# A transformer pair's modulation vectors: from products on TensorE to row sums on ScalarE

## The reference, cut to what matters

```python
c_act = jax.nn.silu(c)                      # (1, 1024)
for l in range(2):
    mod = c_act @ w_ada[l] + b_ada[l]       # (1, 1024) @ (1024, 6144)
    sh1, sc1, g1, sh2, sc2, g2 = jnp.split(mod, 6, axis=-1)
    h = rms_norm(x, ln1_g[l]) * (1.0 + sc1) + sh1
    ...
    x = x + g1 * (merged @ w_out[l])
    ...
```

## Time and profile before

| what | value |
|---|---|
| median of 3 runs | 1462.53 us (1462.26 to 1467.37) |
| the profiled execution | 1466.21 us |
| its span | 1464.4 us |
| TensorE products busy | 1392.3 us, 95% |
| VectorE busy | 872.1 us, 60% |
| ScalarE busy | 802.6 us, 55% |
| GpSimd busy | 547.2 us, 37% |
| granted TensorE clock, mean | 0.974 of full speed |

### The profile page before, as it was taken

How to read it: one execution, slowest core, us unless ns; L and a number is a source line. 1 busy time by engine, 2 the same in 40 slices (tenths; PEclk the granted TensorE clock), 3 DMA queues, 4 the chain that set the end, 5 groups by cost and what they waited for, 6 DMA issues and landing times.

```text
span 1464.4 us, 25774 instructions
## 1 busy us (share of the span) xinstructions
PE 1392.3 (95%) x11032; PEld 1347.1 (92%) x11032; DVE 872.1 (60%) x1047; ACT 802.6 (55%) x954; POOL 547.2 (37%) x249
## 2 busy tenths in 40 slices
PE   6999899998999979999999998999999999899997
PEld 5989899998999979999988997999988998899996
DVE  4865666755555467666759767434445876734443
ACT  4655577765676457777536544454324554455431
POOL 5000288885331337988606000564000600066300
PEclk9999999999899989999999999999999999999998
DMA  7433677777654466777624444555542543355550
GB/s 261 142 115 115 222 275 261 256 292 305 224 207 159 140 239 241 264 262 269 229 103 170 169 145 144 178 191 179 192 150 80 199 155 144 137 192 190 177 198 29
DMA packets 40002, 278.22 MB, mean 190 GB/s; under 512 B 4432, under 2 KB 4560, under 8 KB 8144
## 3 DMA queue, kind: packets, MB, share of 16 engines
q1 hardware_dynamic: 32976, 226.23, 43.8%
q10 hardware_dynamic: 6912, 50.33, 8.9%
HBM read 275.50 MB, written 1.05 MB: 189 GB/s over the span
## 4 chain that ended last, share of the span: by engine, by line
PE 87%; DVE 6%; ACT 3%; POOL 2%; issue 2%; DMA 0%; DVEq 0%; ACTq 0%; SPq 0%; POOLq 0%
PE bank L738 22%; PE bank L740 22%; PE bank L739 22%; PE bank L703 3%; PE bank L704 2%; PE bank L710 2%; DVE low L1421 2%; PE bank L952 1%; PE bank L722 1%; PE bank L724 1%; PE bank L723 1%; PE bank L772 1%; PE bank L759 1%; DVE h L1554 1%; ACT high L1068 1%
## 5 line engine op out<-in xcount | busy, mean ns | idle before, releaser
L1421 DVE TENSOR_TENSOR low<-raw,high 128x2048 fp32r<-128x2048 f32 (+4 forms) x222 | 510.8, 2304 | 306.0 <-ACT high L1068 303.7
L738 PE MATMUL bank<-op_high,low 128*128 128x256 f32 x1904 | 549.1, 288 | 3.3 <-DVE low L1421 3.3
L739 PE MATMUL bank<-op_low,high 128*128 128x256 f32 x1904 | 540.5, 284 | 0.0
L740 PE MATMUL bank<-op_high,high 128*128 128x256 f32 x1904 | 540.4, 284 | 0.0
L1068 ACT ACTIVATE high<-raw 128x2048 fp32r<-128x2048 f32 (+4 forms) x222 | 406.3, 1831 | 155.2 <-PE bank L740 143.6
L738 PEld LDWEIGHTS bank<-op_high,low 128*128 128x128 f32 x1904 | 367.4, 193 | 8.8 <-DVE low L1421 4.4
L739 PEld LDWEIGHTS bank<-op_low,high 128*128 128x128 f32 x1904 | 367.3, 193 | 2.8 <-issue 2.4
L740 PEld LDWEIGHTS bank<-op_high,high 128*128 128x128 f32 x1904 | 367.1, 193 | 0.0
L738 PE MATMUL bank<-act_high,low 128*128 128x256 f32 x864 | 242.7, 281 | 0.0
L740 PE MATMUL bank<-act_high,high 128*128 128x256 f32 x864 | 242.0, 280 | 0.0
L739 PE MATMUL bank<-act_low,high 128*128 128x256 f32 x864 | 240.6, 278 | 0.0
(11 more groups left out here) (288 smaller groups left out, 1910.6 us busy)
## 6 DMA issues: line engine op xcount, KB each, us to landing
raw<-stream SPq DMA_DIRECT2D x198, 1024.0 KB, 4.8
adaw<-ada ACTq DMA_DIRECT2D x48, 1024.0 KB, 6.2
raw<-stream SPq DMA_DIRECT2D x10, 768.0 KB, 4.5
raw<-stream SPq DMA_DIRECT2D x10, 512.0 KB, 3.6
x<-xT SPq DMA_DIRECT2D x1, 1024.0 KB, 5.1
out<-h SPq DMA_DIRECT2D x1, 1024.0 KB, 3.9
raw<-stream SPq DMA_DIRECT2D x2, 384.0 KB, 3.3
consts<-consts_d SPq DMA_DIRECT2D x1, 672.0 KB, 14.1
```

What stands on the lines that cost most here:

```text
L738: pe.matmul(o, wl[:, w], oh[:, k, :], start=one, stop=False, skip_group_check=True)
L739: pe.matmul(o, wh[:, w], ol[:, k, :], start=False, stop=False, skip_group_check=True)
L740: mm = pe.matmul(o, wh[:, w], oh[:, k, :], start=False, stop=end, skip_group_check=True)
L1421: dve.tensor_tensor(low[m % SPLIT][:, 0:w], raw[m % RAW][:, 0:w], high[m % SPLIT][:, 0:w], ALU.subtract).then_inc(S["low_ready"], 1)
```

## The change

The modulation's weights are laid out the other way round on the host: a partition holds one output feature, and a portion two groups of 128 output features by all 1024 input features. The condition's row is loaded once, broadcast to all partitions (`crow`), and silu is applied to the whole row at step 1. GpSimd multiplies each half of a portion by `crow`. Two steps behind, ScalarE copies each half onto itself with a row sum (`accum_out`), which gives 128 finished outputs at a time, in SBUF. VectorE adds the bias from there. The products `ada_sum` on TensorE are gone, with their two borrowed banks.

```diff
-        adas = [sb(f"adas{i}", [P, D], F32, adaln) for i in range(2)]
+        crow = sb("crow", [P, D], F32, adaln)
...
                 if ADA_SUM_AT[seg] == step[0]:
-                    st_("ada_sum", seg), st_("mod", seg)
+                    st_("mod", seg)
             for p in range(48):
+                if ADA_AT[p] + 2 == step[0]:
+                    st_("ada_acc", p)
                 if ADA_AT[p] == step[0]:
+                    if p == 0:
+                        st_("cond_silu")
                     st_("ada", p)
...
             if l == 0:
-                st_("ada_load", 0)
+                st_("ada_cond"), st_("ada_load", 0)
...
-            def ada_sum(seg):
-
-                pe.wait_ge(S["ada_added"], 4 * (seg + 1))
-                bank = MOD_BANK[seg]
-                claim(bank)
-                for b in range(8):
-                    mm = pe.matmul(ps[bank][:, 0, b:b + 1], adas[seg % 2][:, b * P:(b + 1) * P],
-                                   col("ones", 0, 1), start=True, stop=True)
-                mm.then_inc(S["ada_sum"], 1)
-                free_after[bank] = (S["mod_ready"], seg + 1)
...
-            def ffn_in(l):
-                if l == 0:
-                    act.activation(cact[:], col("c"), ACT.Silu).then_inc(S["c_silu"], 1)
+            def ada_cond(_):
+                act.dma_start(crow[:], cond.to_broadcast([P, D])).then_inc(S["c_in"], 16)
+
+            def cond_silu(_):
+                act.wait_ge(S["c_in"], 16)
+                act.activation(crow[:], crow[:], ACT.Silu).then_inc(S["c_silu"], 1)
 
             def ada_load(a):
                 if a >= 3:
-                    act.wait_ge(S["ada_added"], a - 2)
+                    act.wait_ge(S["ada_summed"], 2 * (a - 2))
...
-            def ada_(a):
-
-                act.wait_ge(S[f"ada_in{a % 3}"], 16 * (a // 3 + 1))
-                if a == 0:
-                    act.wait_ge(S["c_silu"], 1)
+            def ada_acc(a):
+
+                l, part, q = a // 24, a // 4 % 6, a % 4
+                w = adaw[a % 3]
                 for i in range(2):
-                    k = 2 * (a % 4) + i
-                    ins = act.activation(adaw[a % 3][:, i, :], adaw[a % 3][:, i, :], ACT.Copy, scale=cact[:, k:k + 1])
-                ins.then_inc(S["ada_scaled"], 1)
+                    act.wait_ge(S["ada_scaled"], 2 * a + i + 1)
+                    m = 8 * part + 2 * q + i
+                    act.activation(w[:, i, :], w[:, i, :], ACT.Copy, accum_out=mod[:, l, m:m + 1])\
+                        .then_inc(S["ada_summed"], 1)
...
                 m = mod[:, l, 8 * part:8 * part + 8]
-                dve.wait_ge(S["ada_sum"], seg + 1)
-                dve.tensor_tensor(m, ps[MOD_BANK[seg]][:, 0, 0:8], col("b_ada", 8 * seg, 8), ALU.add)\
+                dve.wait_ge(S["ada_summed"], 8 * (seg + 1))
+                dve.tensor_tensor(m, m, col("b_ada", 8 * seg, 8), ALU.add)\
                     .then_inc(S["mod_ready"], 1)
...
             def ada_(a):
 
-                seg, part = a // 4, a % 4
-                acc, w = adas[seg % 2], adaw[a % 3]
-                pool.wait_ge(S["ada_scaled"], a + 1)
-                if part == 0:
-                    if seg >= 2:
-                        pool.wait_ge(S["ada_sum"], seg - 1)
-                    pool.tensor_tensor(acc[:], w[:, 0, :], w[:, 1, :], ALU.add).then_inc(S["ada_added"], 1)
-                    return
-                pool.wait_ge(S["ada_added"], a)
-                link(pool.tensor_tensor(acc[:], w[:, 0, :], acc[:], ALU.add))
-                pool.tensor_tensor(acc[:], w[:, 1, :], acc[:], ALU.add).then_inc(S["ada_added"], 1)
+                w = adaw[a % 3]
+                pool.wait_ge(S[f"ada_in{a % 3}"], 16 * (a // 3 + 1))
+                if a == 0:
+                    pool.wait_ge(S["c_silu"], 1)
+                for i in range(2):
+                    pool.tensor_tensor(w[:, i, :], w[:, i, :], crow[:], ALU.mult).then_inc(S["ada_scaled"], 1)
```

More of the change, by code:

```diff
@@ L190, in columns @@
                     ("od_q_gain", 1), ("od_k_gain", 1), ("conv", 2 * 44 * 4), ("ln1", 16), ("ln2", 16),
-                    ("b_ada", 96), ("q_norm", 6), ("kv_norm", 4), ("pool_scale", 8), ("final_g", 8), ("c", 8),
+                    ("b_ada", 96), ("q_norm", 6), ("kv_norm", 4), ("pool_scale", 8), ("final_g", 8),
                     ("w_kr", 512)):
@@ L194, in columns, with build @@
     return where, sizes
-def build(nc, xT, stream, ada, consts_d, params_d, positions, out):
+def build(nc, xT, stream, ada, cond, consts_d, params_d, positions, out):
     CH, _ = linear_chunks()
@@ L232, in build @@
         gmod = sb("gmod", [P, 2, 2, KB])
-        cact = sb("cact", [P, KB])
         small = sb("small", [P, 64])
@@ L336, in build @@
             diff_scores diff_max diff_exp diff_w diff_turned diff_copied diff_pv mix_ready
-            conv_init conv_done silu_done act_mul act_high act_low c_silu ada_in0 ada_in1 ada_in2 ada_scaled ada_added ada_sum mod_ready
+            conv_init conv_done silu_done act_mul act_high act_low c_in c_silu ada_in0 ada_in1 ada_in2 ada_scaled ada_summed mod_ready
             dil_scores dil_max dil_exp dil_w dil_turned dil_copied dil_pv dv_ready
@@ L428, in build @@
         ADA_SUM_AT = [ADA_AT[4 * seg + 3] + 3 for seg in range(12)]
-        MOD_BANK = [NB if 34 <= at < 52 else OB for at in ADA_SUM_AT]
         step = [0]
@@ L445, in conv_stages @@
         def conv_stages(l):
-            st_("norm", 2 * l + 1), st_("ffn_in", l)
+            st_("norm", 2 * l + 1)
             if l == 0:
-                st_("ada_load", 0)
+                st_("ada_cond"), st_("ada_load", 0)
             for j in range(11):
@@ L1041, in _ @@
                           gla_kv=gla_kv, diff_p=diff_p, dil_p=dil_p, dil_p2=dil_p2, mla_p=mla_p,
-                          gla_o=gla_o, diff_s=diff_s, diff_t=diff_t, dil_s=dil_s, dil_t=dil_t, ada_sum=ada_sum, kr=kr_,
+                          gla_o=gla_o, diff_s=diff_s, diff_t=diff_t, dil_s=dil_s, dil_t=dil_t, kr=kr_,
                           krot=krot, wide=wide, qrot=qrot, mla_s=mla_s, mla_t=mla_t)
@@ L1393, in _ @@
                           turns=turns, lam=lam, ar=ar_, la=la_, la_exps=la_exps, ket=ket,
-                          gated=gated, mix=mix, diff_s=diff_s, diff_t=diff_t, dil_s=dil_s, dil_t=dil_t, ffn_in=ffn_in,
-                          silu=silu, ada=ada_, ada_load=ada_load, act=act_, act2=act2, kr=kr_, wide=wide, pool_split=pool_split, y=y_, heads=heads,
+                          gated=gated, mix=mix, diff_s=diff_s, diff_t=diff_t, dil_s=dil_s, dil_t=dil_t, ada_cond=ada_cond, cond_silu=cond_silu,
+                          silu=silu, ada_acc=ada_acc, ada_load=ada_load, act=act_, act2=act2, kr=kr_, wide=wide, pool_split=pool_split, y=y_, heads=heads,
                           after_heads=after_heads,
@@ L1972, in lay_params @@
                       ("q_norm", "q_norm_g_2"), ("kv_norm", "kv_norm_g_2"), ("pool_scale", "pool_scale_2"),
-                      ("final_g", "final_g_2"), ("c", "c_2")):
+                      ("final_g", "final_g_2")):
         put(name, by_feature(i[src]))
@@ L2012 @@
     xT = np.ascontiguousarray(np.asarray(i["x"])[0].T.reshape(KB, P, TOK).transpose(1, 0, 2))
-    wa = np.asarray(i["w_ada_2"]).reshape(2, 4, 2, P, 6, D)
+    wa = np.asarray(i["w_ada_2"]).reshape(2, D, 6, 4, 2, P).transpose(0, 2, 3, 5, 4, 1)
     arrays = {
-        "xT": xT, "stream": lay_stream(i), "ada": np.ascontiguousarray(wa.transpose(0, 4, 1, 3, 2, 5)).reshape(-1),
+        "xT": xT, "stream": lay_stream(i), "ada": np.ascontiguousarray(wa).reshape(-1),
+        "cond": np.ascontiguousarray(np.asarray(i["c_2"]).reshape(1, D)),
         "consts_d": shape_constants(), "params_d": lay_params(i),
```

## The result

The changed kernel takes 1473.31 us (median of 5 runs, 1472.68 to 1473.43) against 1462.53 (5 runs, 1462.08 to 1467.37): a ratio of 1.0061, 95% interval 1.0042 to 1.008. The ratios in this document are those of the means (here 1473.1 and 1464.2). The forecast was 1443.5 us with a range of 1438 to 1453. The profiled execution took 1472.68 us (span 1470.8).

The account below looks back on a forecast made before the run. TensorE, with 87% of the chain, was taken as the bound. 22.0 + 0.7 - 0.1 - 0.4 - 2.0 - 1.0 = 19.2 us saved from 1462.5 gives 1443.3, stated as 1443.5 us, range 1438 to 1453.

Parts of the forecast that it names:

- The 12 blocks: TensorE's 12 blocks of thin `ada_sum` products, 1.78 us each plus or less waits around them: removing them saves 22.0 us.
- the clock: TensorE's granted clock, 0.79 in the 8 us from 395 on, recovers: 0.7 us saved, bounds 0 and 1.5.
- 0.1 and 0.4: Losses from ScalarE's sums coming two steps later: net 0.1 us at step 33's norm, 0.4 us at step 44.
- A product's own cost: A GpSimd product in the modulation must cost what one of its sums does, 2.41 us.
- Rival D: A GpSimd product costs more than a sum, so turns in the `up` steps set TensorE's pace: 1492 us, chance 0.04.
- ScalarE's sum: ScalarE's copy with row sum takes about 1052 ns plus 195 ns to read the accumulator: no change of load.
- The turns: GpSimd and VectorE alternate in `up` steps, falling at worst 0.32 us behind per period; late `act_low` costs TensorE 2.0 us.
- for all such places: ScalarE, held by GpSimd's products before its sums, delays the next splits and so TensorE: 1.0 us, bounds 0 and 9.
- 12 tiny instructions, off the path: VectorE's additions to the modulation, reading the sums from SBUF and not PSUM, were taken to cost nothing.
- no longer waits for ScalarE there: At step 33, GpSimd finishes before VectorE's normalization, which it delayed by 0.9 us; ScalarE's 1.0 us lateness nets 0.1.
- A: GpSimd and VectorE saturate their turns in the `up` steps, costing 6.2 us and not 2.0: 1447.7 us, chance 0.14.
- B: ScalarE's waits reach TensorE where portions stand closest, steps 24-26 and 80-84: 9.6 us, not 1.0; 1452 us, chance 0.14.

Follow-up runs that it names:

- experiment 5: The changed kernel at the old tile addresses, each of GpSimd's 96 products cut to one column of 1024: 1439.24 us, ratio 0.9817 to the kernel before.
- experiment 1: The changed kernel with three unused tiles that put every later tile back at its old address: 1467.55 us, ratio 1.0013 to the kernel before.
- experiment 6: The changed kernel at the old tile addresses, each GpSimd product cut into two of 512 columns: 1459.93 us, ratio 0.9955 to the kernel before.
- experiment 4: The changed kernel with GpSimd's products of each portion held until ScalarE's split of that portion's step: 1475.88 us, ratio 1.0068 to the kernel before.
- experiment 10: The kernel before with unused tiles added and `mod` moved ahead of `x`, putting operands 448 bytes from the weights modulo 512: 1440.32 us, ratio 0.9825.

## Why the prediction was wrong

**Step by step.**
- The 12 blocks and the clock, 22.0 + 0.7, less 0.1 and 0.4, together 22.2: right as far as the runs can tell. With the products reduced to one column the kernel is 26.0 us faster than the kernel before beside it, with 4 to 5 us in it that may be the old sums' own turns (experiment 5). In the `up` and `down` steps the terms agree with the traces to 1.1 us each. L952 is gone, and so are the waits at 395 and 434.
- A product's own cost, like a sum's: right. Its shortest was 2.35 us. Rival D was wrong in its mechanism.
- ScalarE's sum: right, 1048 and 189 ns where 1052 and 195 were taken. Its waits for products, 8.5 us in experiment 1, are not what costs the time (experiment 6).
- The turns: **the step that failed**. The text weighed GpSimd against VectorE over "a period of two `up` steps", 11.84 against 11.52 us, and gave the result 2.0 us for a late `act_low` (bounds 0 and 6.2). That was roughly right: the two waits for `act_low` are 3.6 us in the changed kernel and 3.4 in experiment 1, and the 2 x 22 `up` steps themselves lose 0.6. But the `down` steps were never weighed that way. The working followed one chain of waits there, at the tightest place, found 2 us of slack and took 1.0 us "for all such places, with bounds 0 and 9"; the load over the whole stretch, 42.3 + 23.7 us of turns within the 62, was not added up. There GpSimd has no other work, so nothing holds its products apart, and each keeps VectorE out for its length. The two terms, 3.0 us together, measure 28.3 for all of the products (experiment 5 against 1), and 23 to 24 if the 4 to 5 us are the old sums' turns, which the forecast had in its starting point.
- The same step took the rule of turns from splits alone. The traces show it for the additions of squares and to the modulation too, which have both inputs in SBUF, and the short ones pay most: 0.43 us become 2.5. The kernel before had such additions already (four of 2.5 to 2.6 us), so it could have been read there. One kind was named and priced at nothing ("12 tiny instructions, off the path"): the addition to the modulation, whose input this change moves from PSUM to SBUF, takes 1.62 us on the mean where it took 0.16.
- What had kept the turns apart was, as far as the traces tell, the old dependence; no run shows it, and the hold of experiment 4 didn't bring it back. GpSimd waited 108.8 us (line 1838) and 37.1 us (line 1835) in the kernel before for ScalarE's scaling, and in the `down` steps VectorE worked in those gaps. The forecast saw those waits only as waits to be removed, in the sentence that GpSimd "no longer waits for ScalarE there". Afterwards it waits for transfers alone, 97.3 us, mostly where nothing presses.
- The sum had no term for the addresses: that all other work keeps its pace was assumed without a word. It was 6 to 7 us (experiment 1), outside any part of the kernel that the diff touches.

**The books.** In ratios to the kernel before, of a mean of 1464.2 us: the removal, with the old sums' turns, -0.0183 or -26.8 us (experiment 5; forecast -22.2), the products +0.0196 or +28.7 (experiment 1 less 5; forecast +3.0), the layout +0.0048 or +7.0 (the changed kernel less experiment 1; no term in the forecast). Together +8.9, from 1464.2 to 1473.1. The three parts are differences of the same runs and so add up by construction; each is good to 2 or 3 us.

**The chances.** 0.90 went to a gain, on the strength of a price for the removal that was right. The cost lay between rivals A and B: A's mechanism (turns), B's place (the `down` steps), neither's price.

**What stays open.** Why the same products at the same distance run at 113.4 ns in one stretch and 117.8 in another; and what makes `act_low` late in the faster layout. The 28 us are shown to come from the products' length and to fall in the `down` steps and the mixer; how they divide between the waits for the squares, for `low` and others, and the clock behind them, is read from one trace each. That taking products away from the `down` steps by another schedule would give the removal's 22 us in full was not tried.

## What to carry to other kernels

Before work is given to an idle GpSimd, list every VectorE instruction with two SBUF inputs in the same stretch, the short ones first, and charge each with the length of one GpSimd instruction; do so where GpSimd has nothing else to do, not only where it is busy. A wait that a change takes away may have been what kept two engines out of each other's way (argued from the traces here, not shown by a run). Cut the shared work to the length at which the fixed cost and the waits balance (here 512 columns: 1459.9 us against 1467.6 with 1024 and 1481.5 with 256), and compare a change with its tiles held at their old addresses, or an accident of the layout is counted with it.

## What the runs showed of the hardware

- The spacing of products of 256 columns at the full clock depends on where operand and weights lie in SBUF. With the operand 0 or 256 bytes from the weight tiles (modulo 512) it was 119.5 to 120.0 ns in every stretch; at 288 it was 116.7 to 117.9 by stretch, at 384 118.7 and at 480 118.3; at 64, 192, 320 and 448 it was about 113.4 or about 117.8, in stretches of tens of us and more that keep one of the two. Moving tiles by a few columns made the unchanged computation 1.75% faster (experiment 10).
- A VectorE addition of 0.43 us took 0.9, 1.45 and 2.5 us beside GpSimd instructions of 256, 512 and 1024 columns.
- GpSimd's product took at shortest 0.71, 1.25 and 2.35 us for 256, 512 and 1024 columns: by a line through these three, an estimate, some 0.17 us of each is fixed.
